# The last six tiles of a shared expert as three rounded products, with their sums weighed by GpSimd

## The reference, cut to what matters

```
routed = routed_experts(x, idx, wts, w_gate, w_up, w_down)
shared = (silu(x @ shared_w_gate) * (x @ shared_w_up)) @ shared_w_down
f = routed + shared
x = x + g2 * rmsnorm(f, post_ffn_g)
```

## Time and profile before

| what | us |
|---|---|
| median of 3 runs | 1740.5 |
| lowest, highest | 1740.08, 1745.26 |
| the profiled execution's own time | 1741.91 |
| its span | 1740.2 |
| PE (TensorE) busy | 1604.6 |
| DVE (VectorE) busy | 1124.4 |
| ACT (ScalarE) busy | 899.8 |
| POOL (GpSimd) busy | 607.8 |

### The profile page before, as it was taken

The page is one execution under the profiler, slowest core; times in us unless marked ns, Lnnn a source line. Parts: engine busy times, 40 slices in busy tenths (PEclk is TensorE's granted clock), DMA queues, the critical chain, the costliest instruction groups (busy, mean ns, idle before and its releaser), DMA issues.

```text
span 1740.2 us, 26456 instructions
## 1 busy us (share of the span) xinstructions
PE 1604.6 (92%) x8785; PEld 1160.7 (67%) x8786; DVE 1124.4 (65%) x1575; ACT 899.8 (52%) x1389; POOL 607.8 (35%) x555
## 2 busy tenths in 40 slices
PE   5999999679889898776999999999999999999997
PEld 4555555333336666634888888888888888888843
DVE  3255566552224556467788878778788788778746
ACT  1011111142335655415677777777777777777733
POOL 0055676500000000013344554544454554555310
PEclk8999999869999999877999999999999999999999
DMA  9688867577774211575899999999999999999884
GB/s 340 210 260 296 284 216 226 161 261 241 225 235 146 79 55 44 196 282 190 297 310 321 318 317 324 319 324 334 325 333 336 330 327 338 331 325 341 278 254 186
DMA packets 156010, 457.45 MB, mean 263 GB/s; under 512 B 25374, under 2 KB 35805, under 8 KB 138457
## 3 DMA queue, kind: packets, MB, share of 16 engines
q1 hardware_dynamic: 119289, 368.12, 58.9%
q0 software_dynamic: 26624, 69.80, 15.9%
q10 hardware_dynamic: 9960, 17.83, 3.0%
HBM read 394.52 MB, written 78.15 MB: 272 GB/s over the span
## 4 chain that ended last, share of the span: by engine, by line
PE 43%; DVE 5%; DMA 4%; ACT 2%; issue 2%; POOL 0%; POOLq 0%; ACTq 0%; DVEq 0%
PE ps L2398 12%; PE ps L2358 8%; PE ps L2377 8%; DMA acc_d<-yb,tokb 4%; PE ps L2336 4%; PE ps L2360 4%; PE ps L2735 2%; PE ps L2363 1%; DVE lo_dn L2433 1%; PE ps L2753 1%; DVE lo_gu L2433 1%; PE ps L1863 1%; PE ps L2362 1%; DVE xT_h L2440 0%; ACT xT_h L2253 0%
## 5 line engine op out<-in xcount | busy, mean ns | idle before, releaser
L2433 DVE TENSOR_TENSOR lo_gu<-raw_gu,hi_gu 128x1024 fp32r<-128x1024 f32 x256 | 301.9, 1221 | 53.5 <-ACT hi_gu L2246 53.0
L2358 PE MATMUL ps<-xT_h,hi_gu 128*128 128x416 f32 (+4 forms) x896 | 269.6, 364 | 4.8 <-DVE xT_h L2440 3.4
L2246 ACT ACTIVATE hi_gu<-raw_gu 128x1024 fp32r<-128x1024 f32 x256 | 255.3, 1048 | 0.0
L2195 POOL DMA_INDIRECT acc_d<-yb,tokb x96 | 159.2, 1659 | 245.1 <-ACT yb L2299 233.3
L602 PE MATMUL ps<-w_in_sb,hT 128*128 128x512 f32 x512 | 226.6, 601 | 1.1 <-ACT hT L466 1.1
L2360 PE MATMUL ps<-xT_h,lo_gu 128*128 128x208 f32 (+4 forms) x896 | 225.0, 251 | 0.0
L446 POOL TENSOR_TENSOR prod<-kring,qbc 128x512 f32<-128x512 f32 x128 | 161.9, 1297 | 174.5 <-DMA kring<-in_cache_k 121.1
L2175 POOL DMA_INDIRECT xg<-h_d,tokb x96 | 137.0, 1427 | 168.3 <-PE ps L2336 129.9
L602 PEld LDWEIGHTS ps<-w_in_sb,hT 128*128 128x128 f32 x512 | 97.0, 192 | 119.5 <-issue 118.1
L2358 PEld LDWEIGHTS ps<-xT_h,hi_gu 128*128 128x128 f32 x896 | 169.3, 189 | 9.1 <-DVE xT_h L2440 3.8
L2398 PE MATMUL ps<-hi_dn,hT_h 128*128 128x512 f32 (+5 forms) x512 | 170.4, 400 | 3.0 <-DVE hb_l L2473 2.9
(11 more groups left out here) (362 smaller groups left out, 3005.6 us busy)
## 6 DMA issues: line engine op xcount, KB each, us to landing
raw_gu<-in_expert_w_gate SPq DMA_DIRECT2D x64, 1024.0 KB, 9.9
raw_gu<-in_expert_w_up SPq DMA_DIRECT2D x64, 1024.0 KB, 14.1
raw_dn<-in_expert_w_down SPq DMA_DIRECT2D x64, 1024.0 KB, 10.1
kring<-in_cache_k SPq DMA_DIRECT2D x128, 256.0 KB, 3.3
vring<-in_cache_v SPq DMA_DIRECT2D x128, 256.0 KB, 2.9
adaw<-in_ada_w ACTq DMA_DIRECT2D x7, 2048.0 KB, 12.9
adaw<-in_ada_w SPq DMA_DIRECT2D x5, 2048.0 KB, 15.0
w_in_sb<-in_w_in SPq DMA_DIRECT2D x4, 2048.0 KB, 19.9
```

The source lines that it names most:

```text
L2195: pool.indirect_dma_start(out=acc_d[b % 2][:, :], out_offset=bass.IndirectOffsetOnAxis(ap=tokb[0:rows, b:b + 1], axis=0), in_=yb[b % 2][0: ...
L2246: act.activation(hi_cut(n, u), raw_cut(n, u), ACT.Copy).then_inc(hi_made, 1)
L2358: pe.matmul(ps[:, bank, 0:2 * cap], wh, x[:, k, :, :].rearrange("p a t -> p (a t)"), start=(k == 0), stop=False)
L2433: dve.tensor_tensor(lo_cut(n, u), raw_cut(n, u), hi_cut(n, u).bitcast(F32), ALU.subtract).then_inc(lo_made, 1)
```

## The change

The shared weights become expert n = 64 (NE): they are loaded into the raw buffers of the routed experts and split in the last pair, cuts 0 to 3 in the stages where the next pair's would be, cuts 4 and 5 at the pair's end. The hidden tiles are split too: the first two by ScalarE and VectorE in front of ScalarE's last eviction, the other four inside the end, high part on ScalarE, rest on GpSimd. The turned hidden rows are split by ScalarE and VectorE. Each of the six tiles' products becomes three rounded ones; the gate/up of the next tile is halved around the turn of this one. GpSimd does the multiplication by the gate for all but the last tile. Five of the nine inputs are loaded once the last product of the experts is done, ahead of the wait for the scatters, and the other four behind the first six pairs of sums. Several buffers are placed elsewhere; these lines are left out, and the overflow's too.

```diff
-            return [(n, u) for n, u in of if n < NE]
+            return of
...
+        for u in (4, 5):
+            nth_cut[NE, u] = len(nth_cut) + 1
...
-            sp.wait_ge(dn_mm, last_block(NE - 4) + 1)
+            sp.wait_ge(gu_mm, turn_of(NE - RAWS))
+            for h, w in enumerate((sw_gate, sw_up)):
+                sp.dma_start(raw_gu[NE % RAWS][:, h, :], w[0].rearrange("(p k) f -> p (k f)", k=KC)).then_inc(gu_in[NE % RAWS], 16)
+            sp.wait_ge(dn_mm, last_block(NE - RAWS) + 1)
+            sp.dma_start(raw_dn[NE % RAWS][:, :, :], sw_down[0].rearrange("(c p) n -> p c n", p=P)).then_inc(dn_in[NE % RAWS], 16)
+            sp.wait_ge(dn_mm, last_block(NE + 1 - RAWS) + 1)
             for t in SH:
                 sp.dma_start(hx2[t - NWIN][:, :, :], h2T_d[t].rearrange("p (k t) -> p k t", k=KC)).then_inc(hx2_in[t - NWIN], 16)
-            sp.wait_ge(dn_mm, last_block(NE - 3) + 1)
-            for h, w in enumerate((sw_gate, sw_up)):
-                sp.dma_start(s_gu2[:, h, :], w[0].rearrange("(p k) f -> p (k f)", k=KC)).then_inc(sw2_in, 16)
-            sp.dma_start(s_dn2[:, :, :], sw_down[0].rearrange("(p c) n -> p c n", c=FC)).then_inc(sw2_in, 16)
...
                 evict(3 * p + 1)
+            round_weights([(NE, 4), (NE, 5)])
+            for u in range(2):
+                round_hidden(act, u)
             evict(MAIN - 1)
+
+        def round_hidden(act, u):
+            act.wait_ge(hx2_in[u], 16)
+            if u >= 2:
+                act.wait_ge(gu6, u - 1)
+                act.wait_ge(hx2_lo_made, u - 1)
+            else:
+                act.wait_ge(x_tr, MAIN)
+            act.activation(hx2_hi[u % 2][:, :, :], hx2[u][:, :, :], ACT.Copy).then_inc(hx2_hi_made, 1)
+
+        def rest_of_hidden(eng, u):
+            eng.wait_ge(hx2_hi_made, u + 1)
+            eng.tensor_tensor(hx2_lo[u][:, :, :], hx2[u][:, :, :], hx2_hi[u % 2][:, :, :].bitcast(F32), ALU.subtract
+                              ).then_inc(hx2_lo_made, 1)
...
+            rest_of_weights([(NE, 4), (NE, 5)])
+            for u in range(2):
+                rest_of_hidden(dve, u)
...
+            sp.wait_ge(dn_mm, MAIN)
+            sp.wait_ge(o_ended, 1)
+            for q in range(5):
+                load_input(q)
             for j in range(2):
                 sp.wait_ge(rows_out[j], 16 * (MAIN // 2))
-            sp.wait_ge(o_ended, 1)
...
             for q in range(A1):
                 load_sums(q)
-                load_input(q)
-            for q in range(A1, T9):
+            for q in range(5, T9):
                 load_input(q)
...
             gated(NWIN)
+            turned(NWIN)
+            round_hidden(act, 2)
+            gated(NWIN + 1)
             for q, t in enumerate(SEQ_T):
-                if t not in SH:
-                    hidden_of(SEQ_T[q + 1])
-                elif q and SEQ_T[q - 1] in SH:
-                    hidden_of(t)
                 norm(q)
+                if t in SH:
+                    if t + 1 in SH:
+                        turned(t + 1)
+                    if t + 2 in SH:
+                        gated(t + 2)
+                    if t + 3 in SH:
+                        round_hidden(act, t + 3 - NWIN)
...
+                for k in ks:
+                    for x, w in ((hx2_hi[u % 2], hi_gu[NE % 2]), (hx2_hi[u % 2], lo_gu[NE % RAWS]), (hx2_lo[u], hi_gu[NE % 2])):
...
+            gate_up(NWIN, range(KC))
             for t in SH:
                 if t + 1 < T9:
-                    gate_up(t + 1)
-                turn_down(t)
+                    gate_up(t + 1, range(KC // 2))
+                turn(t)
+                if t + 1 < T9:
+                    gate_up(t + 1, range(KC // 2, KC))
+                down(t)
...
+        def finish_pool(pool):
+            for q in range(T9 - 1):
+                u = 2 + q // 2
+                if q % 2 == 0 and NWIN + u in SH:
+                    rest_of_hidden(pool, u)
+                pool.wait_ge(summed, q + 1)
+                weigh(pool, q)
...
+            def rest_of_turned(t):
+                u = t - NWIN
+                dve.wait_ge(hT6_hi, u + 1)
+                dve.tensor_tensor(hT6[u % 2][:, 1].rearrange("p c t -> p (c t)"), ps[:, u % 2, 0:F],
+                                  hT6[u % 2][:, 0].rearrange("p c t -> p (c t)").bitcast(F32), ALU.subtract).then_inc(hT6_here, 1)
...
             hidden(NWIN)
+            rest_of_turned(NWIN)
+            hidden(NWIN + 1)
             for q, t in enumerate(SEQ_T):
-                if t in SH and t + 1 in SH:
-                    hidden(t + 1)
                 if q == T9 - 1:
                     finish(q - 1)
                 total(q)
+                if t + 1 in SH and t in SH:
+                    rest_of_turned(t + 1)
                 if 0 < q < T9 - 1:
                     finish(q - 1)
+                if t + 2 in SH and t in SH:
+                    hidden(t + 2)
             finish(T9 - 1)
```

More of the change, by code:

```diff
@@ L2056, in build @@
         wslot = [place(f"wslot{j}", 207 + j / 32, [P, 1]) for j in range(6)]
-        s_gu2 = place("s_gu2", 89, [P, 2, KC * F])
-        s_dn2 = place("s_dn2", 105, [P, FC, D])
         x1_5 = [place(f"x1_5{j}", 113 + 4 * j if j < 6 else 41 + 4 * (j - 6), [P, D]) for j in range(T9)]
-        sw2_in = sem("sw2_in")
         SH = range(NWIN, T9)
-        hx2 = [place(f"hx2_{j}", 65 + 4 * j, [P, KC, P]) for j in range(T9 - NWIN)]
+        hx2 = [place(f"hx2_{j}", 89 + 4 * j, [P, KC, P]) for j in range(T9 - NWIN)]
+        hx2_lo = [place(f"hx2_lo{j}", 89 + 4 * j, [P, KC, P], F32R) for j in range(T9 - NWIN)]
+        hx2_hi = [place(f"hx2_hi{j}", 25 + 4 * j, [P, KC, P], F32R) for j in range(2)]
+        hx2_hi_made, hx2_lo_made = sem("hx2_hi_made"), sem("hx2_lo_made")
         hx2_in = [sem(f"hx2_in{j}") for j in range(T9 - NWIN)]
@@ L2627, in build @@
         SEQ_T = [1, 3, 2, 4, 0, 5, 6, 7, 8]
[L2628 to L2635 removed]
+        a0 = [place(f"a0_{j}", 161 + 4 * j, [P, D]) for j in range(A0)]
+        a1 = [place(f"a1_{j}", kb, [P, D]) for j, kb in enumerate((189, 193, 197, 201, 53, 57))]
+        sg6 = [place(f"sg6_{j}", 6 + j, [P, F]) for j in range(2)]
+        h6 = [place(f"h6_{j}", 8 + j, [P, F]) for j in range(2)]
+        hT6 = [place(f"hT6_{j}", 61 + 2 * j, [P, 2, FC, P], F32R) for j in range(2)]
+        hT6_hi = sem("hT6_hi")
+        junk6 = place("junk6", 33, [P, D])
+        g2s = place("g2s", 2, [NS, D])
+        s6 = [place(f"s6_{j}", 10 + j / 32, [P, 4]) for j in range(2)]
         g2s_in = sem("g2s_in")
@@ L2696, in turned @@
                     act.wait_ge(dn6, u - 1)
[L2697 removed]
+                act.activation(hT6[u % 2][:, 0].rearrange("p c t -> p (c t)"), ps[:, u % 2, 0:F], ACT.Copy).then_inc(hT6_hi, 1)
             def norm(q):
@@ L2726, in finish_act, with gate_up @@
                 norm(q)
+                if t in SH:
[5 more added lines that the diff above has]
+                        round_hidden(act, t + 3 - NWIN)
         def finish_pe(pe):
-            def gate_up(t):
+            def gate_up(t, ks):
                 u = t - NWIN
-                pe.wait_ge(hx2_in[u], 16)
-                if u >= 2:
-                    pe.wait_ge(hT6_here, u - 1)
-                for k in range(KC):
-                    last = pe.matmul(ps[:, u % 2, :].rearrange("p (a f) -> p a f", a=2), hx2[u][:, k, :],
-                                     s_gu2[:, :, k * F:(k + 1) * F], start=(k == 0), stop=(k == KC - 1))
-                last.then_inc(gu6, 1)
@@ L2739, in turn_down @@
-            def turn_down(t):
+                if ks[0] == 0:
+                    pe.wait_ge(hx2_lo_made, u + 1)
+                if u == 0 and ks[0] == 0:
+                    pe.wait_ge(lo_made, nth_cut[NE, 3])
+                    pe.wait_ge(hT_made, turn_of(NE - 1))
+                if u >= 2 and ks[0] == 0:
+                    pe.wait_ge(hT6_here, u - 1)
+                for k in ks:
+                    for x, w in ((hx2_hi[u % 2], hi_gu[NE % 2]), (hx2_hi[u % 2], lo_gu[NE % RAWS]), (hx2_lo[u], hi_gu[NE % 2])):
+                        first = k == 0 and x is hx2_hi[u % 2] and w is hi_gu[NE % 2]
+                        last = pe.matmul(ps[:, u % 2, :].rearrange("p (a f) -> p a f", a=2), x[:, k, :],
+                                         w[:, :, k * F:(k + 1) * F], start=first, stop=(k == KC - 1 and x is hx2_lo[u]))
@@ L2740, in turn_down, with turn @@
+                if ks[-1] == KC - 1:
+                    last.then_inc(gu6, 1)
+            def turn(t):
                 u = t - NWIN
@@ L2751, in turn_down, with weigh @@
                 for half in range(2):
+                    cols = slice(512 * half, 512 * half + 512)
                     for ch in range(FC):
-                        last = pe.matmul(ps[:, 4 + 2 * (u % 2) + half, :], hT6[u % 2][:, ch, :],
-                                         s_dn2[:, ch, 512 * half:512 * half + 512], start=(ch == 0), stop=(ch == FC - 1))
```

(19 more changed lines are left out.)

37 lines of the change are left out of this document (12 added, 25 removed).

## The result

The changed kernel took 1749.6 us in the median of 9 runs (1746.03 to 1754.71), the kernel before, on the same chip, 1741.4 us (1739.22 to 1746.54, 9 runs): a ratio of 1.004 with a 95% interval of 1.0026 to 1.0054. Between the medians it is 8.2 us slower, by the ratio 7.0. The forecast was 1746.4 us, slower at 0.50, range 1734.5 to 1750.5.

A forecast was written before the change was run, and what follows sets the result against it. Today's tail was taken as PE-bound. Sums at 1678.0, then 8.5, rounds 14.1 + 14.1 + 11.5 + 7.8 and 11.3 gave 1745.3; with 0.8 for the clock, +5.9 on the median: 1746.4 us, range 1734.5 to 1750.5.

The forecast's parts named there:

- The cheaper products: Six shared tiles: rounded gate/up 5.45 us, down 2.72; saves 13.5 us of PE if PE stays the bound.
- The last pair: Six more weight cuts: PE stalls 1.5 us, last eviction starts at 1663.8, first gate/up at 1664.5, 2.1 us later.
- The sums: First addition of loaded sums, 14.3 us behind the last eviction's start: 1678.0, bounds 1675.5 and 1679.5.
- lays them over the last scatter: Five input loads (2.5 MB) moved ahead leave the sums but overlap the last scatter; 1678.0 kept for the sums.
- The work moved to POOL: Eight weighings and four subtractions at 2.4 us each, some 3.5 to 3.7 where they meet DVE at the shared port.
- The rounds: Start of one down product to the next, from tile 4, with DVE waiting for POOL: 14.1, 14.1, 11.5, 7.8 us.
- the path from the first sum to the first down product: Addition 1.2, POOL's weighing 2.4, two additions 2.5, ACT 1.9, rest 0.4: 8.5 us, to 1686.5.
- The last down product: Follows 4.9 us without matmuls; half clock costs 2.7 more, 1.2 hidden; 0.8 taken from 0 to 1.5 us.
- The table loads: ACT's table switches: next instruction 1.30 us after the load's start; a drain would make the estimate about 3 us longer.
- The additions: Arithmetic of the forecast's terms: 11.5 us for tile 7's round, 11.3 behind the start of the last down product.
- Rival 3: Tail: first sums late (1679.5) and clock falls in 3 us gaps before gate/ups, +9 to +10: 1750 us; chance 0.10.
- Rivals 1 and 2: Tail: 1, no real POOL/DVE conflict, 5.4 us faster, chance 0.16; 2, PE stays the bound, 12 us faster, 0.06.

The follow-up runs named there:

- inputs_late: Changed kernel with the nine input loads back where they were, one behind each pair of sums, none ahead of the last scatter: 1748.4 us, ratio 1.0035.
- the two variants of the kernel before: Kernel before plus twelve unused GpSimd operations: products that read SBUF, 1755.5 us, ratio 1.0059; memsets that only write, 1740.9 us, ratio 0.9975.
- pool_idle: Changed kernel with weighings and hidden-tile subtractions both back on VectorE, GpSimd idle behind the scatters: 1747.2 us, ratio 1.0014.
- warm: Changed kernel with 18, 6, 6 and 18 idle matmuls before the down products of tiles 4, 5, 6 and 8: 1751.8 us, ratio 1.0043.
- rest_on_vector: Changed kernel with the four hidden-tile subtractions back on VectorE, GpSimd keeping the eight weighings: 1751.7 us, ratio 1.0043.

## Why the prediction was right, and where it was off

Direction and mechanism were right, and the median lies in the range, 3.2 us above the number. Measured from the anchor the forecast was 1745.3 + 0.8 - 1645.6 = 100.5 us; it was 103.3.

- **The cheaper products**: right. 24 and 12 matmuls take 5.45 and 2.72 us at full clock, and PE stopped being the bound, as said. In the changed kernel none of the 13.5 us saved reached the end.
- **The last pair**: right. The stall was 1.38 us (1.5 forecast), the last eviction started at anchor + 18.1 (18.2 forecast, 16.6 before), the first gate/up at anchor + 18.8 (18.9).
- **The sums**: this is the term that was mis-sized. I kept 1678.0, anchor + 32.4, bounds to + 33.9; it was + 36.0. The step that failed is "lays them over the last scatter", for which I took nothing. The scatter's 128 rows ran beside 2.1 MB of inputs (four loads of 512 KB and one of 32; the forecast's 2.5 MB was a slip) and landed after 8.5 us in place of 6.2, shown by inputs_late (6.2 us, sums 2.8 us sooner). Some 0.8 of the 3.6 is in the sums' own loads and stays open.
- **The work moved to POOL**: right, price and meeting. 2.34 to 2.41 us alone (2.4 forecast), 3.2 to 3.4 when it meets DVE (3.5 to 3.7). By the Trainium skill (SBUF — State Buffer, Who interferes with whom) a VectorE instruction with two SBUF inputs contends with a GpSimd instruction that reads SBUF and not with one that only writes; the two variants of the kernel before bear out both halves (3.18 us against 1.28).
- **The rounds**: 13.5, 13.4, 11.4 and 7.8 us against 14.1, 14.1, 11.5 and 7.8. The waits stand where they were foretold, at the multiply-add for the subtraction and at the first addition for the weighing, and are 1.9 to 2.2 us each (3.21 - 1.28, 3.42 - 1.22), not 2.4. With the path from the first sum to the first down product (8.35 us, 8.5 forecast) 1.6 us less in sum. That path was right in part by luck: the 2.4 us put down for POOL's weighing were 1.33 of waiting for the next pair of sums and 1.02 at the port.
- **The last down product**: I took 0.8 us out of 0 to 1.5 for the clock. It ran 2.8 us longer (5.50 against 2.72) and DVE waited 1.73 for it, beyond the bound. The other slow down products (5.0, 4.6, 4.4 us) cost nothing by themselves, since DVE reached the sum later than PE. 0.9 us more.
- **The table loads**: ACT's next instruction started 1.29 or 1.30 us after each load that it directly followed, eight of the nine, so the 1.3 us of the earlier trace rows held, and the 3 us that the forecast names for a drain did not come.
- **The additions**: the terms behind the last down product add up to 11.45 us, not 11.3, and tile 7's to 11.6, not 11.5; some 0.2 us in sum, which changes nothing.

3.6 - 1.6 + 0.9 = 2.9, the 2.8 that are missing up to rounding. So the total is nearer than its parts: too little for the sums and the clock, too much for the rounds. Rival 3 foretold just these two (late sums, slow products in the gaps) and 1750 us, though the sums came later than its 1679.5 (anchor + 33.9), and the clock fell behind shorter pauses than its 3 us: 1.9 us before two down products. Its effects came on top of GpSimd's work, which by the square of variants (anchor to end: both kinds of work on GpSimd 103.3, one of them 101.8 and 99.6, none 96.8) is the largest single item: 67.3 - 61.2 = 6.1 us behind the first sum. That is net of the 12 operations that VectorE is spared. Some 5 us of it are turns at the port; 1.2 us are GpSimd's own length, 2.38 us where VectorE takes 1.22, in front of tile 8's gate/up, where the chain runs through the subtraction. Rivals 1 and 2 fell with the rounds of over 13 us.

How the 8.7 us divide: 5.2 in front of the first sum (1.5 the last pair's split, 3.6 the loads), 3.5 behind it, where the 2.6 that pool_idle saves against the kernel before (63.8 - 61.2) are set against the 6.1 of GpSimd's work.

## What to carry to other kernels

Before work is handed to an idle GpSimd, list what VectorE does at that moment: if both read SBUF with two inputs, an operation of GpSimd that VectorE meets costs it nearly the whole length, more than to do the work itself (1.9 to 2.2 us of wait here against 1.24 of work). No run here had a GpSimd operation that reads one input. A cheaper product helps only where TensorE stays the bound; look at what is behind it in the round. And a load moved ahead "into idle time" is to be held against the transfer that the path waits for.

## What the runs showed of the hardware that I had not expected

- A clock drop is not cured for certain by filling the pause in which it showed. With idle matmuls before four down products the granted clock fell behind two pauses that were left (2.25 and 2.48 us), and at tile 8 PE kept half speed for some 3.4 us although it was then busy all the time. With eight matmuls more it stayed at 1.00, with two pauses of that length (2.50 and 2.47 us) still left.
- Whether it falls differs from run to run. The pause before the first gate/up product is 1.97 to 2.02 us in the changed kernel and its ten variants. Behind it the 36 matmuls took 8.5 us in six of them and 10.1 us, part of it at a granted clock of 0.5, in five. So one execution each doesn't show that the filling moved the drop; it shows what a drop costs where it lies on the path, 1.6 us.
- A slow TensorE can hide a slow TensorE: in the changed kernel the down product of tile 6 ran slow, at no cost, and so left only 1.06 us of pause before the next; where it ran fast (inputs_late, warm) the pause grew to 2.4 us and the slow stretch moved onto the path.
- Operations on 8 partitions pay the same at the port as those on 128: the weighing of tile 0 took 3.36 us (8x1024) where it had to wait, 2.39 where it started first (rest_on_vector).
